# Differential attention on one core: each half of the second map gets its own shift and factor, and the score scale moves into the queries

## What is computed

```python
sc = jnp.einsum('bqhmd,bkhmd->bmhqk', qb, k).astype(jnp.float32) * scale + bias[None, None]
p = jax.nn.softmax(sc, axis=-1)
a = p[:, 0] - lam * p[:, 1]
return jnp.einsum('bhqk,bkhd->bqhd', a.astype(v.dtype), v)
```

## Time and profile before

| what | value |
|---|---|
| median of 3 runs | 4045.36 us (4042.28 to 4050.85) |
| the profiled execution | 4044.97 us |
| its span, first to last instruction | 4043.2 us |
| busy, whole span: PE, DVE, ACT, POOL | 3793.2, 2236.1, 1658.7, 2286.1 us |
| mean granted clock of PE | 0.982 |

### The profile page before, as it was taken

The page is one execution under the profiler, slowest core; times in us unless marked ns, Lnnn a source line. Parts: engine busy times, 40 slices in busy tenths (PEclk is TensorE's granted clock), DMA queues, the critical chain, the costliest instruction groups (busy, mean ns, idle before and its releaser), DMA issues. The chain is left out here.

```text
span 4043.2 us, 51539 instructions
## 1 busy us (share of the span) xinstructions
PE 3793.2 (94%) x19002; PEld 2624.1 (65%) x19002; DVE 2236.1 (55%) x3973; ACT 1658.7 (41%) x2886; POOL 2286.1 (57%) x1381
## 2 busy tenths in 40 slices
PE   8999999999989999889989999999999899998898
PEld 8789774555546666557777897755555466665577
DVE  3003125555569999875531030255556699998755
ACT  3102103333348888760031021033333488887610
POOL 1221325877768888744512213267777688886455
PEclk9999999999999999999989999999999999999999
DMA  5433445233420222245354334422233202223353
GB/s 176 126 132 118 145 134 123 62 82 71 91 59 1 57 57 58 57 112 190 130 174 130 128 120 140 144 68 55 66 73 77 59 1 57 57 58 72 109 177 135
DMA packets 180864, 392.43 MB, mean 97 GB/s; under 512 B 18014, under 2 KB 100168, under 8 KB 168968
## 3 DMA queue, kind: packets, MB, share of 16 engines
q1 hardware_dynamic: 179752, 387.75, 34.3%
q10 hardware_dynamic: 864, 1.41, 0.2%
HBM read 255.93 MB, written 135.67 MB: 97 GB/s over the span
## 5 line engine op out<-in xcount | busy, mean ns | idle before, releaser
L1297 POOL TENSOR_TENSOR mla_sum_pool<-mla_sum_pool,mla_probs 128x1024 f32<-128x1024 f32 (+1 forms) x336 | 777.8, 2315 | 209.0 <-ACT mla_probs L1258 184.2
L1315 DVE TENSOR_REDUCE carry_row_max<-psum 128x1 f32<-128x512 f32 x688 | 474.2, 689 | 416.1 <-PE psum L1130 411.2
L1258 ACT ACTIVATE mla_probs<-psum 128x1024 f32<-128x1024 f32 x384 | 373.3, 1021 | 694.4 <-PE psum L1167 689.7
L1690 DVE TENSOR_REDUCE diff_row_max<-psum 128x1 f32<-128x1024 f32 x512 | 613.4, 1217 | 49.6 <-PE psum L1534 38.9
L1613 ACT ACTIVATE diff_probs<-psum,diff_shift 128x1024 f32<-128x1024 f32 x512 | 566.1, 1111 | 178.0 <-DVE diff_shift L1697 171.8
L1560 PE MATMUL psum<-ident,diff_probs 128*128 128x128 f32 x2048 | 328.1, 284 | 93.0 <-DVE diff_turned L1724 80.9
L638 PE MATMUL psum<-in_x_hi,in_w_hi 128*128 128x512 f32 x1024 | 409.4, 400 | 2.7 <-ACT in_mla_val L745 2.7
L638 PE MATMUL psum<-in_x_hi,in_w_lo 128*128 128x512 f32 x1024 | 405.5, 396 | 0.0
L638 PE MATMUL psum<-carry_firsts,in_w_hi 128*128 128x512 f32 x1024 | 404.5, 395 | 0.0
L1560 PEld LDWEIGHTS psum<-ident,diff_probs 128*128 128x128 f32 x2048 | 215.9, 141 | 265.0 <-issue 254.3
L1671 POOL TENSOR_TENSOR diff_probs<-diff_probs 128x1024 f32<-128x1024 f32 x128 | 305.8, 2389 | 141.6 <-ACT diff_probs L1621 141.3
(11 more groups left out here) (213 smaller groups left out, 7363.7 us busy)
## 6 DMA issues: line engine op xcount, KB each, us to landing
in_w_raw<-in_w_in SPq DMA_DIRECT2D x64, 512.0 KB, 3.9
split_d<-in_out SPq DMA_DIRECT2D x64, 512.0 KB, 2.7
raw_d<-in_out SPq DMA_DIRECT2D x32, 512.0 KB, 2.7
mq_d<-in_out SPq DMA_DIRECT2D x48, 256.0 KB, 3.6
mk_d<-in_out SPq DMA_DIRECT2D x48, 256.0 KB, 4.0
carry_firsts<-split_d SPq DMA_DIRECT2D x48, 256.0 KB, 8.1
carry_weights<-split_d SPq DMA_DIRECT2D x48, 256.0 KB, 7.7
carry_weights<-split_d SPq DMA_DIRECT2D x16, 768.0 KB, 18.1
```

Source lines behind the costliest of these rows:

```text
L1258: nc.scalar.activation(probs[:, s % RING, :].rearrange("p (a n) -> p a n", n=CH), psum[:, S0 + 2 * (s % 2):S0 + 2 * (s % 2) + 2, :], ACT.E ...
L1297: nc.gpsimd.tensor_tensor(acc, start, probs[:, s % RING, mine], ALU.add).then_inc(pool_added, 1)
L1315: nc.vector.tensor_reduce(row_max[:, u % 2, qb, n:n + 1], psum[:, sweep_bank(g), :], AX.X, ALU.max).then_inc(maxed, 1)
L1690: nc.vector.tensor_reduce(row_max[:, n % 2, m, half:half + 1], banks(n, m, half), AX.XY, ALU.max).then_inc(maxed, 1)
```

## The change

Three things change, and the order of the work on each engine stays.

1. The score scale is multiplied into the queries where the input projection writes them out (`tile_scale`; on DVE one instruction for each of these tiles becomes a multiply-subtract), and the bias tables for this attention are made without its inverse. The exponential's own scale goes.
2. For map 1, each half has its own shift, the negated maximum of that half (`part_shift`), which the maximum instruction writes directly (`negate=True`). The exponential of a half waits for its own maximum instead of for the shift of both. The shift of the whole map is still made, as the smaller of the two.
3. So each half of map 1 has a correction factor, exp(shift of the whole - shift of the half), a new ACT instruction on 128x2 (`parts`). `ratios` multiplies the two row sums by it, and gives a factor for each half (128x2), by two more DVE instructions: the product of sums and factors (`weighed`), and the first map's sum times lambda (`first_lam`). ACT and POOL use the factor of the half at hand.

```diff
 @@ input_projection, ScalarE and VectorE @@
-                            nc.scalar.activation(out[:, s, :].bitcast(F32R), tile_banks(g), ACT.Copy).then_inc(tile_out, 1)
+                            nc.scalar.activation(out[:, s, :].bitcast(F32R), tile_banks(g), ACT.Copy, scale=tile_scale(t)
+                                                 ).then_inc(tile_out, 1)
...
+                        if T_DQ <= t < T_DK:
+                            nc.vector.scalar_tensor_tensor(out[:, s, :].bitcast(F32R), tile_banks(g), DIFF_SCALE,
+                                                           out[:, slot_of["high", g], :], ALU.mult, ALU.subtract
+                                                           ).then_inc(tile_lo, 1)
+                            continue
 @@ diff_attention, ScalarE @@
-                def exp(n, m):
-                    act.wait_ge(shifted, 2 * n + m + 1)
-                    if m == 0 and n >= DEEP:
-                        act.wait_ge(turn_done, 4 * (n - DEEP + 1))
-                    if m == 1 and n >= DEEP1:
-                        act.wait_ge(mixed, 2 * (n - DEEP1 + 1))
+                def exp(n, m, half):
+                    if m == 0:
+                        act.wait_ge(shifted, 2 * n + 1)
+                        bias = shift[:, n % 2, 0:1]
+                        if n >= DEEP:
+                            act.wait_ge(turn_done, 4 * (n - DEEP + 1))
+                    else:
+                        act.wait_ge(maxed, 4 * n + 2 + half + 1)
+                        bias = part_shift[:, n % 2, half:half + 1]
+                        if n >= DEEP1:
+                            act.wait_ge(mixed, 2 * (n - DEEP1 + 1))
...
+                def parts(n):
+                    act.wait_ge(shifted, 2 * n + 2)
+                    nc.scalar.activation(part[:, n % DEEP1, :], part_shift[:, n % 2, :], ACT.Exp,
+                                         bias=shift[:, n % 2, 1:2], scale=-1.0).then_inc(parted, 1)
...
                     if on:
-                        exp(n, 1)
+                        exp(n, 1, 0)
+                        exp(n, 1, 1)
+                        parts(n)
 @@ diff_attention, VectorE @@
+                    if n >= 2:
+                        dve.wait_ge(parted, n - 1)
+                    nc.vector.tensor_reduce(part_shift[:, n % 2, half:half + 1], banks(n, m, half), AX.XY, ALU.max,
+                                            negate=True).then_inc(maxed, 1)
...
                     dve.wait_ge(exped, 4 * (n + 1))
+                    dve.wait_ge(parted, n + 1)
+                    nc.vector.tensor_tensor(row_sum[:, n % 2, 1, :], row_sum[:, n % 2, 1, :], part[:, n % DEEP1, :],
+                                            ALU.mult).then_inc(weighed, 1)
+                    dve.wait_ge(weighed, n + 1)
                     nc.vector.tensor_reduce(totals[:, :, qb, h], row_sum[:, n % 2, :, :], AX.X, ALU.add
                                             ).then_inc(summed, 1)
                     dve.wait_ge(summed, n + 1)
                     nc.vector.reciprocal(inv1[:, n % 2:n % 2 + 1], totals[:, 1, qb, h:h + 1]).then_inc(inverted, 1)
+                    nc.vector.tensor_scalar(first_lam[:, n % 2:n % 2 + 1], totals[:, 0, qb, h:h + 1], dots[:, 0:1], None,
+                                            ALU.mult).then_inc(lam_ready, 1)
                     dve.wait_ge(inverted, n + 1)
+                    dve.wait_ge(lam_ready, n + 1)
                     if n >= 2:
                         dve.wait_ge(times_ratio, 2 * (n - 1))
-                    nc.vector.tensor_scalar(ratio[:, n % 2:n % 2 + 1], inv1[:, n % 2:n % 2 + 1],
-                                            totals[:, 0, qb, h:h + 1], dots[:, 0:1], ALU.mult, ALU.mult
-                                            ).then_inc(ratio_ready, 1)
+                        dve.wait_ge(act_scaled, n - 1)
+                    nc.vector.tensor_scalar(ratio[:, n % 2, :], part[:, n % DEEP1, :], inv1[:, n % 2:n % 2 + 1],
+                                            first_lam[:, n % 2:n % 2 + 1], ALU.mult, ALU.mult).then_inc(ratio_ready, 1)
```

More of the change, by code:

```diff
@@ L1609, in exp @@
                     dst = probs[:, n % DEEP, :] if m == 0 else probs1[:, n % DEEP1, :]
-                    if m == 0 and n >= 2:
+                    if n >= 2:
                         act.wait_ge(summed, n - 1)
[L1612 to L1615, removed]
+                    nc.scalar.activation(dst[:, half * HALF:(half + 1) * HALF].rearrange("p (a n) -> p a n", n=CH),
+                                         banks(n, m, half), ACT.Exp, bias=bias,
+                                         accum_out=row_sum[:, n % 2, m, half:half + 1]).then_inc(exped, 1)
@@ L1617, in scale @@
+                def parts(n):
+                    act.wait_ge(shifted, 2 * n + 2)
+                    nc.scalar.activation(part[:, n % DEEP1, :], part_shift[:, n % 2, :], ACT.Exp,
+                                         bias=shift[:, n % 2, 1:2], scale=-1.0).then_inc(parted, 1)
                 def scale(n):
                     act.wait_ge(ratio_ready, n + 1)
-                    at = 0 if n < LATE else HALF
-                    first = probs1[:, n % DEEP1, at:at + CH]
-                    nc.scalar.activation(first, first, ACT.Copy, scale=ratio[:, n % 2:n % 2 + 1]).then_inc(act_scaled, 1)
+                    half = 0 if n < LATE else 1
+                    first = probs1[:, n % DEEP1, half * HALF:half * HALF + CH]
+                    nc.scalar.activation(first, first, ACT.Copy, scale=ratio[:, n % 2, half:half + 1]
+                                         ).then_inc(act_scaled, 1)
@@ L1646, in _ @@
                     if on:
-                        exp(n, 0)
+                        exp(n, 0, 0)
+                        exp(n, 0, 1)
                     if n == UNITS:
@@ L1663, in _ @@
                     pool.wait_ge(ratio_ready, n + 1)
-                    at = 0 if n < LATE else HALF
                     done = 2 * n if n < LATE else LATE + n
[L1666 to L1680, removed]
+                    for k, half in enumerate((0, 1) if n < LATE else (1,)):
+                        at = slice(half * HALF, (half + 1) * HALF)
+                        rest = probs1[:, n % DEEP1, half * HALF + (CH if k == 0 else 0):(half + 1) * HALF]
+                        nc.gpsimd.tensor_scalar(rest, rest, ratio[:, n % 2, half:half + 1], 1.0, ALU.mult, ALU.mult
+                                                ).then_inc(times_ratio, 1)
+                        if k == 0:
+                            pool.wait_ge(act_scaled, n + 1)
+                        pool.wait_ge(times_ratio, done + k + 1)
+                        nc.gpsimd.tensor_tensor(probs[:, n % DEEP, at], probs[:, n % DEEP, at],
+                                                probs1[:, n % DEEP1, at], ALU.add).then_inc(mixed, 1)
                 pool.wait_ge(o_ready, (H - 1) * (NB // 2))
@@ L2468, in constants @@
     kb, qb = np.arange(NB)[:, None], np.arange(NB)[None, :]
-    far = f32(1.0 / DIFF_SCALE)
-    left, right = (kb <= qb - 2) * far, (kb >= qb + 2) * far
+    left, right = kb <= qb - 2, kb >= qb + 2
     lo_rows = (np.arange(2 * NB) >= NB).astype(f32)
```

40 lines of the change are left out of this document (27 added, 13 removed).

## The result

| | median us | lowest to highest | runs |
|---|---|---|---|
| before | 4047.28 | 4042.28 to 4050.85 | 4 |
| changed | 4125.02 | 4122.46 to 4130.30 | 4 |

The ratio is 1.0195, with a 95% interval of 1.0177 to 1.0212: the change makes the kernel 78 us slower. The forecast was 4071 us, 26 us slower, in a range of 4052 to 4088. The sign was right and the time lies outside the range. One execution of a later run, the added product with two inputs, took 11097 us at a granted clock of 0.371 against 0.98; its median of four counts it, its ratio doesn't.

What follows compares the result with a forecast made beforehand. A loop through PE and DVE was taken to bound the kernel; 0.35 us a stretch, less room, gave +32.6 us for both stages, earlier exponentials -7, so 4045.4 + 26 = 4071 us, range 4052 to 4088.

Steps and rivals of the forecast that it cites:

- (a): In `ratios` on DVE: the new 128x2 product goes ahead of L1706's counterpart, which waits for it, +0.19 us a stretch.
- (c): In `ratios`: the factor waits for `first_lam`, step 0.25 us where the reciprocal's was 0.20, +0.05; its four waits, +0.03.
- The room and the count of stretches: 64 stretches a stage, each from L1706's start to the next DVE copy; slack absorbs 5.4 us a stage, the first two 0.7.
- the sum: Both differential stages: 64 stretches times the added time, less 0.7 and 5.4 us, twice, less 7 us for earlier exponentials.
- The relief of PE's scores: Map 1's earlier exponentials spare PE's scores 0.17 us in each of 18 to 19 quick even rounds a stage, -7 us for both.
- Rival 1: On DVE: both new instructions cost only their place in the queue, 0.12 to 0.2 us; +1 to +8 us, no change; chance 0.14.
- Rival 2: On DVE: waits and queue stalls make the chain 0.45 to 0.5 us longer a stretch; +38 to +44 us; chance 0.20.
- Rival 3: Map 1's earlier exponentials free PE's scores in all 32 even rounds a stage, DVE costing next to nothing; -11 us; chance 0.06.
- the four waits: On the factor in `ratios`: four waits in place of two, priced at +0.03 us a stretch as a middle value.

Runs made afterwards that it cites:

- the two-instruction product: Changed kernel with the 128x2 product of sums and factors written as two 128x1 DVE instructions, one SBUF tensor and a pointer scalar each: 4095.46 us, ratio 1.0128.
- the kernel without block: Changed kernel in which GpSimd scales and adds only 512 of the 1024 columns of its second piece: 4072.07 us, ratio 1.0066.
- the kernel that has nothing else: Changed kernel without `parts`, product and `first_lam`, factor written as 128x1, so only the early exponentials stay: 4040.63 us, ratio 0.9987 against before.

## Why the prediction was wrong

**The step that failed** is the first of the chain, "(a) the product of sums and factors on 128x2 ... +0.19". I priced it by a row of a lone product ahead of the loop. In the loop it stands beside GpSimd's pass, and when the two overlap it ends when GpSimd's instruction ends: 0.15 us when it is free, up to 1.75 us when not, 45.8 us too long in all. With it failed the reason for pricing GpSimd's delay at nothing, that "POOL starts later too, but it waits over a microsecond for ACT in each round". The room was there, but the product ties the factor to the end of GpSimd's pass, and the pass waits for the factor. What ran side by side now runs in line: 6.6 us of GpSimd's work, 0.6 of its wait for ACT (36.5 us over 64 rounds) and 1.2 of its wait for the factor (91.8 less the first 18.3, over 63), 8.3 us in sum. From one factor to the next it is 8.38 us on average in the steady part of the first stage, and was 7.75 before. PE's transposes wait 73 us a stage for what GpSimd adds.

**The other steps, one by one.** Before, the steps from L1706 to the maximum were 0.57 us; unblocked they are now 0.95 (1332.89 to 1333.84), so +0.38 for a forecast of +0.35. The product's reader starts 0.19 us behind it (0.19 forecast). `first_lam` starts 0.08 behind the reciprocal (0.08). From it to the factor 0.29 us pass, where the two terms (c) made 0.28. The room and the count of stretches agree with two runs: the sum gave 51 us for the two-instruction product (52 measured) and 26 for the kernel without block (25 to 27). The relief of PE's scores, -7, came as -5 (-7 by the medians) in the kernel that has nothing else; the first stage had 16 gaps of 0.55 us between transposes and scores, where the prediction counted 18 to 19, and one is left. `parts` on ACT, put at some 0.2 us, takes 0.30.

**The rivals.** Rival 1 (it hides): only an unread instruction that isn't blocked hides, 3 us or nothing for 128 of them. Rival 2 (a dearer chain) has the sign, but 4125 us lies outside its 4083 to 4089, and its mechanism is not what happened: the four waits cost what I gave them. Rival 3 (faster) fell for this kernel; its gain is real but is 5 to 7 us, not 11.

**What no rival held.** I asked of each new instruction what it waits for by semaphore and how long it is, and not whether it and GpSimd want the same access to SBUF. In the part of the trace of before that I read, nothing is blocked: DVE's instructions in the steady loop were reductions, 128x1 operations with one SBUF tensor, copies out of PSUM, and L1742, whose second input is in PSUM. But the trace of before did show the block elsewhere. In the latent attention four equal instructions with two SBUF tensors on 32x16 numbers take 0.22, 0.22, 2.27 and 2.31 us; the two long ones start while GpSimd runs, and each ends 0.03 us after GpSimd's sum (here 648.06 + 2.37 = 650.43 and 648.19 + 2.27 = 650.46):

```profile
L1382 DVE SCALAR_TENSOR_TENSOR mla_far_acc<-mla_sides,mla_far,mla_far_acc x4: 221/1248/2310, 647.4 to 650.6; 32x16 f32<-32x16 f32 x4
```

```profile
648.06 2.37 POOL L1297 TENSOR_TENSOR mla_sum_pool<-mla_sum_pool,mla_probs 128x1024 f32<-128x1024 f32 x1 [1.79 <-ACT mla_probs L1258]
648.19 2.27 DVE L1382 SCALAR_TENSOR_TENSOR mla_far_acc<-mla_sides,mla_far,mla_far_acc 32x16 f32<-32x16 f32 x1
```

These rows show an instruction of the new product's form, two SBUF tensors, beside a running GpSimd instruction. The row that I took the earlier trace rows shows it where GpSimd has nothing to do.

## What to carry to other kernels

Where GpSimd runs long instructions beside DVE, look at the kind of each DVE instruction before its size: one of 128x2 float32 numbers with two SBUF inputs, or with one SBUF input and two columns, can take as long as what is left of GpSimd's instruction, and if GpSimd waits for its result the two engines run in line. A sum made of step lengths holds only if the row for each step ran beside the same neighbours. A group of small instructions of one shape whose shortest, median and longest differ widely (146/428/1751 ns here) may be blocked and not at work, and no list of waits names it: compare its ends with GpSimd's. What helped here was to write it with one column and the second operand as a per-partition scalar, or to give it to ACT, which had room.

## What the runs showed of the hardware

- One column against two in a `tensor_scalar` from SBUF to SBUF is the difference between never stretched (139/143/145 ns, 124 of 128 beside a running GpSimd instruction) and blocked (157/498/1942 ns), and between no change and 62 us of the kernel.
- A two-column factor whose tensor input is one column read twice is blocked as well (286/403/1842 ns).
- A per-partition scalar read from SBUF doesn't count as a second SBUF input: 256 products took 197 to 208 ns, 242 of them started while GpSimd ran.
- In the changed kernel the 128x2 factor takes 285 to 292 ns in all rounds. It could be blocked by its form (with two one-input products ahead of it, two of 128 were stretched, the longest to 1297 ns), but it stands behind the product, and none of the 128 starts while GpSimd runs.
- GpSimd is held up by DVE in turn. In the kernel before, once in each differential stage, a DVE instruction of 128x1024 with two SBUF tensors starts 0.16 us before GpSimd's sum, and that sum takes 3.33 us. The other 126 sums of this line take 2.34 to 2.40 us:

```profile
1682.77 1.27 DVE L1731 SCALAR_TENSOR_TENSOR diff_probs<-diff_probs,diff_ratio 128x1024 f32<-128x1024 f32 x1
1682.93 3.33 POOL L1671 TENSOR_TENSOR diff_probs<-diff_probs 128x1024 f32<-128x1024 f32 x1
```

```profile
L1671 POOL TENSOR_TENSOR diff_probs<-diff_probs x128: 2338/2374/3335, 1198.0 to 3696.4; 128x1024 f32<-128x1024 f32 x128
```
